# Two expert routers: the inverse root leaves the gathered rows, places come from two matmuls, and the first weight pieces are split before the router

## The reference, cut to what matters

```python
def rms_norm(x, g):                                   # first mixture's norm; the second's is the same
    return x * lax.rsqrt(jnp.mean(x * x, axis=-1, keepdims=True) + 1e-6) * g

# first mixture: 4 groups of 8 experts, width 512; a row picks one group and two experts in it
g_logit = h @ w_rg + b_rg;  g_sel = argmax(g_logit);  g_p = softmax(g_logit)[g_sel]
e_logit = (h @ w_re + b_re) of that group;  top_v, top_i = top_k(e_logit, 2)
gate = softmax(top_v) * g_p
out[row] += gate * ((silu(h @ w_gate[e]) * (h @ w_up[e])) @ w_down[e])

# second mixture: 8 experts, width 2816; two of them per row
logits = h @ router_w + router_b;  top_v, top_i = top_k(logits, 2);  gate = softmax(top_v)
out += gate[e] * ((silu(h @ w1[e]) * (h @ w3[e])) @ w2[e])
```

## Time and profile before

| | |
|---|---|
| median of 3 runs | 2421.14 us (2418.27 to 2421.76) |
| profiled execution, its own time | 2415.43 us |
| its span | 2413.6 us |
| PE busy, share of the span | 95% |
| DVE busy | 76% |
| ACT busy | 61% |
| mean DMA rate | 256 GB/s over the span |

### The profile page before, as it was taken

The page is one execution under the profiler, slowest core; times in us unless marked ns, Lnnn a source line. Parts: engine busy times, 40 slices in busy tenths (PEclk is TensorE's granted clock), DMA queues, the critical chain, the costliest instruction groups (busy, mean ns, idle before and its releaser), DMA issues.

```text
span 2413.6 us, 30101 instructions
## 1 busy us (share of the span) xinstructions
PE 2303.7 (95%) x12162; PEld 1877.1 (78%) x12162; DVE 1828.2 (76%) x1897; ACT 1479.5 (61%) x1469; POOL 28.7 (1%) x33
## 2 busy tenths in 40 slices
PE   7989998999999998988999998899999999999997
PEld 6777877888888887776788776678888888888885
DVE  5875658888888887766454577687988878888885
ACT  5345537777777776545443654477776767777765
POOL 0100000000000000010000001000000000000000
PEclk9989998999999999999999999899999999999999
DMA  9434445999999997606455551279999989999991
GB/s 231 129 108 149 151 158 192 363 366 358 369 355 369 355 370 251 208 4 199 155 194 170 167 164 62 83 256 362 355 358 367 357 298 348 359 365 356 367 342 65
DMA packets 281223, 617.57 MB, mean 256 GB/s; under 512 B 31849, under 2 KB 130409, under 8 KB 243697
## 3 DMA queue, kind: packets, MB, share of 16 engines
q1 hardware_dynamic: 279664, 611.33, 73.5%
q10 hardware_dynamic: 1408, 4.19, 0.4%
HBM read 612.34 MB, written 1.05 MB: 254 GB/s over the span
## 4 chain that ended last, share of the span: by engine, by line
PE 86%; DVE 9%; ACT 4%; issue 2%; DMA 0%; DVEq 0%; ACTq 0%; SPq 0%
PE ps L569 25%; PE ps L570 25%; PE ps L571 24%; DVE ring_parts L593 3%; PE ps L2162 1%; ACT high_parts L589 1%; PE ps L2843 1%; PE ps L2132 1%; PE ps L3132 1%; PE ps L2133 1%; DVE arena L3389 1%; PE ps L2176 0%; PE ps L675 0%; PE ps L2177 0%; PE ps L1082 0%
## 5 line engine op out<-in xcount | busy, mean ns | idle before, releaser
L593 DVE TENSOR_TENSOR ring_parts<-ring,high_parts 128x2048 fp32r<-128x2048 f32 (+1 forms) x574 | 1283.1, 2274 | 172.7 <-ACT high_parts L589 172.2
L589 ACT CAST high_parts<-ring 128x2048 fp32r<-128x2048 f32 (+1 forms) x574 | 1078.6, 1897 | 185.3 <-PE ps L571 181.1
L571 PE MATMUL ps<-high_parts,arena_parts 128*128 128x512 f32 (+2 forms) x1560 | 618.5, 396 | 0.0
L569 PE MATMUL ps<-high_parts,hT_parts 128*128 128x512 f32 (+2 forms) x1120 | 455.7, 407 | 28.2 <-DVE ring_parts L593 9.8
L570 PE MATMUL ps<-ring_parts,hT_parts 128*128 128x512 f32 (+2 forms) x1120 | 444.2, 397 | 0.0
L569 PE MATMUL ps<-high_parts 128*128 128x512 f32 x912 | 365.2, 400 | 0.0
L570 PE MATMUL ps<-ring_parts,high_parts 128*128 128x512 f32 x912 | 359.3, 394 | 0.0
L571 PE MATMUL ps<-high_parts 128*128 128x512 f32 x912 | 356.5, 391 | 0.0
L571 PEld LDWEIGHTS ps<-high_parts,arena_parts 128*128 128x128 f32 x1560 | 298.9, 192 | 68.7
L569 PE MATMUL ps<-high_parts,arena_parts 128*128 128x512 f32 x744 | 294.5, 396 | 7.2 <-DVE arena_parts L1878 2.9
L570 PE MATMUL ps<-ring_parts,arena_parts 128*128 128x512 f32 x744 | 293.8, 395 | 0.0
(11 more groups left out here) (533 smaller groups left out, 1791.3 us busy)
## 6 DMA issues: line engine op xcount, KB each, us to landing
ring<-in_moe_w SPq DMA_DIRECT2D x248, 1024.0 KB, 5.2
ring<-in_w_gate SPq DMA_DIRECT2D x64, 1024.0 KB, 5.5
ring<-in_w_up SPq DMA_DIRECT2D x64, 1024.0 KB, 5.4
ring<-in_w_down SPq DMA_DIRECT2D x64, 1024.0 KB, 5.3
ring<-in_w_in SPq DMA_DIRECT2D x104, 256.0 KB, 4.4
ring<-in_ffn_w SPq DMA_DIRECT2D x44, 512.0 KB, 4.9
ring<-in_w_in SPq DMA_DIRECT2D x20, 1024.0 KB, 5.7
ring<-in_moe_w SPq DMA_DIRECT2D x32, 512.0 KB, 5.0
```

The costliest lines, as they stand in the source:

```text
L569: pe.matmul(dst, a_hi, b_hi, start=first, stop=False, skip_group_check=True)
L571: return pe.matmul(dst, a_lo, b_hi, start=False, stop=last, skip_group_check=True)
L589: act.copy(high_flat(p), raw_flat(p)).then_inc(upper, 1)
L593: dve.tensor_tensor(raw_flat(p, ring_parts_flat), raw_flat(p), f32(high_flat(p)), ALU.subtract).then_inc(split, 1)
```

## The change

In words:

- ACT's copy `m_xh` and DVE's `m_xl` are made from `x*g` without `rstd`, one half of the columns at a time: `upper_rows_act` and `lower_rows_dve`, each two instructions of 128x512 per half. The left half is done before the last add into `x`, the right half after it.
- `rstd` is multiplied into both gates (`two_gates`), and stands as one more column of `gate_w`, so that the small gate matmuls bring it to the gathered rows; Silu takes it as its scale. For the very first step two further small matmuls bring it, ahead of the gates.
- The running counts take two matmuls and four small DVE operations; the count of the fullest bucket is made after the selection (`count_dve`).
- In `gather` the three chunks that open the banks do all their high products first, a row tile at a time, so that they can start before the low rows are there; `up` waits for each chunk of rows as it needs it, not for all eight.
- The first two weight pieces of each expert layer are split before the router: on ACT at the places where the hooks of the output projection stand, on DVE one after q = 1 (second layer: before q = 0) and one between the adds q = 2 and q = 3 (`behind`). The high buffers are dealt out in another order so that these are free in time.
- After the last add DVE multiplies by the gain first and copies the transposes after it; ACT squares first and copies after it. In the second router a quarter of the router's matmuls (row tile 1 of the left half) stands behind the last transposes.

The core of the diff:

```diff
@@ evacuate
                         copy(j, ps[:, j.bank, 0:j.n]).then_inc(evac_act if engine == "act" else evac_dve, 1)
+                        if behind:
+                            behind(eng, j)
@@ first_act: out_hook
                 if i == n_ab + 13 and phase:
                     moe_gain_act(act, moe1)
+                    act.wait_ge(used, pieces_of["out_1"][1].n + 1)
+                    split_high(act, moe1.plan[0].up[0])
                 if i == n_ab + 14 and phase:
                     evac_half(act, "act", "n2", g2T, None, 0, (2, 3))
-                    norm_half_act(act, 0)
+                    act.wait_ge(used, pieces_of["out_1"][2].n + 1)
+                    split_high(act, moe1.plan[0].up[1])
+                    norm_half_act(act, 0, nt_squares)
+                    upper_rows_act(act, moe1, 0)
@@ first_dve
+                if i == n_ab + 13 and phase:
+                    split_low(dve, moe1.plan[0].up[0])
+            def out_behind(dve, j):
+                if j.q == 2:
+                    split_low(dve, moe1.plan[0].up[1])
+                    lower_rows_dve(dve, moe1, 0)
-            evacuate(dve, "out_1", "dve", lambda j, src: out_copy(dve, j, src), hook=out_hook)
+            evacuate(dve, "out_1", "dve", lambda j, src: out_copy(dve, j, src), hook=out_hook, behind=out_behind)
+            dve.wait_ge(evac_dve, jobs_of["out_1"][-1].evac)
+            moe_gained_dve(dve, moe1, 1)
             evac_half(dve, "dve", "n2", g2T, None, 1, (6, 7))
-            moe_gained_dve(dve, moe1, 1)
@@ router_pe
-            for t in range(NT):
-                pe.matmul(ps[:, 6, t * nb:(t + 1) * nb], causal_up[:], r_hit[:, t, 0:nb], start=True, stop=(t == 0))
-                if t:
-                    pe.matmul(ps[:, 6, t * nb:(t + 1) * nb], ones[:], r_hit[:, t - 1, 0:nb], start=False, stop=True)
-            for t in range(NT):
-                mm = pe.matmul(ps[:, 6, NT * nb:(NT + 1) * nb], ones[:], r_hit[:, t, 0:nb], start=(t == 0), stop=(t == NT - 1))
-            mm.then_inc(sig("placed"), 1)
+            pe.matmul(upto, causal_up[:], hit, start=True, stop=True)
+            pe.matmul(total, ones[:], hit, start=True, stop=True).then_inc(sig("placed"), 1)
@@ place_dve
+            dve.tensor_copy(r_place[:, 1, 0:nb], total[:, 0, :])
+            vstep(dve, dve.tensor_tensor(r_place[:, 0, 0:nb], upto[:, 0, :], r_hit[:, 0, 0:nb], ALU.mult))
+            vstep(dve, dve.tensor_tensor(r_place[:, 1, 0:nb], r_place[:, 1, 0:nb], upto[:, 1, :], ALU.add))
+            vstep(dve, dve.tensor_tensor(r_place[:, 1, 0:nb], r_place[:, 1, 0:nb], r_hit[:, 1, 0:nb], ALU.mult))
@@ two_gates
+            vstep(dve, dve.tensor_tensor(r_c[:, 7], r_c[:, 7], rstd[:], ALU.mult))
             vstep(dve, dve.tensor_tensor(r_c[:, 8], r_c[:, 7], r_c[:, 5], ALU.mult))
...
+            for t in range(NT):
+                dve.tensor_copy(gate[:, t, :, f.e], rstd[:, t:t + 1].to_broadcast([P, f.buckets]))
+                first, second = [oh[:, t].rearrange("p (b k) -> p b k", k=f.e) for oh in (oh1, oh2)]
+                ins = dve.tensor_tensor(gate[:, t, :, 0:f.e], first, second, ALU.add)
@@ router_norm_act, and the new functions
-            norm_half_act(act, 1)
+            norm_half_act(act, 1, nt_squares)
+            evac_half(act, "act", PLAIN[f.number - 1], g2T if f is moe1 else gain_of(1, 1), None, 1, (6, 7) if f is moe1 else (2, 3))
             norm_root_act(act, n)
-            act.wait_ge(sig("rstd"), n + 1)
+            upper_rows_act(act, f, 1)
+        def upper_rows_act(act, f, half):
+            cols = slice(512 * half, 512 * half + 512)
+            act.wait_ge(sig("moe_xg"), 4 * (f.number - 1) + 2 * half + 2)
             for t in range(NT):
-                act.wait_ge(sig("moe_xg"), 4 * f.number)
-                ins = act.mul(m_xh[:, t, :], nt_xn[:, t, :], rstd[:, t:t + 1])
-            ins.then_inc(sig("moe_xh"), 1)
+                act.copy(m_xh[:, t, cols], nt_xn[:, t, cols]).then_inc(sig("moe_xh"), 1)
+        def lower_rows_dve(dve, f, half):
+            cols = slice(512 * half, 512 * half + 512)
+            for t in range(NT):
+                dve.wait_ge(sig("moe_xh"), 4 * (f.number - 1) + 2 * half + t + 1)
+                dve.tensor_tensor(m_xl[:, t, cols], nt_xn[:, t, cols], f32(m_xh[:, t, cols]), ALU.subtract).then_inc(sig("moe_xl"), 1)
@@ moe_main_pe: gather
-                pe.wait_ge(sig("moe_sel"), k + 1)
-                pe.wait_ge(sig("moe_xl"), f.number)
...
+                for t in range(NT):
+                    pe.wait_ge(sig("moe_xh"), 4 * (f.number - 1) + 2 + t + 1)
+                    pe.wait_ge(sig("moe_sel"), NT * k + t + 1)
+                    for c in range(3):
+                        upper(c, t)
+                if b == 0:
                     for t in range(NT):
+                        pe.matmul(ps[:, TURN, 0:1], f32(m_sel[:, t, 0:P]), rstd[:, t:t + 1], start=(t == 0), stop=(t == NT - 1))
+                for t in range(NT):
+                    pe.wait_ge(sig("moe_xl"), 4 * (f.number - 1) + 2 + t + 1)
+                    for c in range(3):
+                        lower(c, t)
+                for c in range(3, KC):
+                    pe.wait_ge(sig("moe_rows"), KC * k + c - 2)
+                    for t in range(NT):
+                        upper(c, t)
+                        lower(c, t)
@@ moe_main_pe: up
+                    if gathered is not None:
+                        pe.wait_ge(sig("moe_rows"), KC * gathered + c + 1)
@@ moe_main_act: silu
-                act.activation(m_sg[:, 0:st.n], ps[:, GATE, 0:st.n], ACT.Silu).then_inc(sig("moe_silu"), 1)
...
+                act.activation(m_sg[:, 0:st.n], ps[:, GATE, 0:st.n], ACT.Silu, scale=scale).then_inc(sig("moe_silu"), 1)
@@ moe_main_dve
             select(0)
+            lower_rows_dve(dve, f, 1)
+            count_dve(dve, f)
@@ out_part (second router)
                     if slot == 7 and l:
-                        router_half_pe(pe, moe2, 0)
+                        router_half_pe(pe, moe2, 0, (0,))
...
                     turn_half(pe, x, 1, (2, 3))
+                    router_half_pe(pe, moe2, 0, (1,))
...
+                def behind(dve, j):
+                    if l and j.q == 2:
+                        lower_rows_dve(dve, moe2, 0)
+                        split_low(dve, moe2.plan[0].up[1])
```

More of the change, by code:

```diff
@@ L627, in pe_project, with evacuate @@
                         each(pe, j)
[L629 removed]
+        def evacuate(eng, name, engine, copy=None, norm=None, hook=None, x_done=None, behind=None):
             if norm is not None:
@@ L723, in norm_whole_act, with norm_half_act @@
             ins.then_inc(sig("norm_sq"), 1)
-        def norm_half_act(act, half):
+        def norm_half_act(act, half, squares=None):
             for t in range(NT):
                 cols = slice(half * 512, (half + 1) * 512)
-                ins = act.activation(nt_sq[:, t * 512:(t + 1) * 512], x[:, t, cols], ACT.Square, accum_out=half_sums[half][:, t:t + 1])
+                sq = nt_sq[:, t * 512:(t + 1) * 512] if squares is None else squares[:, t, cols]
+                ins = act.activation(sq, x[:, t, cols], ACT.Square, accum_out=half_sums[half][:, t:t + 1])
             if half:
@@ L974, in emit @@
         group_m.high_at = spare - 2 * PIECE
+        M_HIGH = [0, 0, 0]
+        for k in range(3):
+            M_HIGH[(n_ab + 13 + k) % 3] = spare - k * PIECE
         def highs(*starts):
             return [high_parts[:, a - HI_BASE:a - HI_BASE + PIECE] for a in starts]
-        group_m.high = highs(spare, spare - PIECE, spare - 2 * PIECE)
+        group_m.high = highs(*M_HIGH)
         for l in range(LAYERS):
@@ L1554, in emit, with router_half_pe @@
         assert MR.at <= MR_AT + MR_SIZE
-        def router_half_pe(pe, f, half):
+        def router_half_pe(pe, f, half, tiles=(0, 1)):
             w, n = (r1_w, 36) if f is moe1 else (r2_w, NE2)
             xT_ready(pe, PLAIN[f.number - 1], half)
-            for t in range(NT):
+            for t in tiles:
                 for c in range(4 * half, 4 * half + 4):
@@ L1734, in emit @@
         m_rows = [(e_hT, e_hT_lo)] + [tuple(a[:, :, q, :] for a in m_rows3) for q in range(TOGETHER - 1)]
-        moe1.group.high = moe2.group.high = [MX.take(PIECE) for _ in range(HIGH)]
+        lot = [MX.take(PIECE) for _ in range(HIGH)]
+        moe1.group.high = moe2.group.high = [lot[k] for k in (2, 1, 0, 3, 4)]
         MF = Arena(arena)
@@ L2025, in moe_act_bucket @@
                 act.wait_ge(*m.at("gu", g * f.steps + k + 1))
-                act.activation(e_sg[:, k % 2, :], ps[:, 2 + k % 2, 0:FB], ACT.Silu).then_inc(m("silu"), 1)
+                act.wait_ge(*m.at("places", g + 1))
+                act.activation(e_sg[:, k % 2, :], ps[:, 2 + k % 2, 0:FB], ACT.Silu, scale=e_gate[:, f.e:f.e + 1]).then_inc(m("silu"), 1)
                 act.wait_ge(*m.at(f"down{f.slots[k]}_ready", 16 * (g * f.fills[f.slots[k]] + f.nth[k])))
@@ L2267, in rows @@
```

(4 more changed lines are left out.)

120 lines of the change are left out of this document (69 added, 51 removed).

## The result

The changed kernel took **2427.24 us** (median of 11 runs, 2424.51 to 2430.84), the kernel before beside it 2421.10 (11 runs, 2413.39 to 2422.48): ratio 1.0032 [1.0022, 1.0041], slower by 0.3%. Forecast were 2426.1 and a range of 2420.5 to 2429.5. Its profiled execution took 2425.64 us, span 2423.9.

What follows compares the result with a forecast made beforehand. PE was taken to bound the expert streams, and its waits for small things the routers. Second layer's start +4.95, second gather +0.6, first router -0.5 sum to +5.05 us: 2426.1 us, range 2420.5 to 2429.5.

Steps and rivals of the forecast that it cites:

- The late add, +3.8 and +2.2: Second router: q = 3's add comes late, last transposes start +3.8 us later; lower clock from there to the logits, +2.2.
- Logits to gather, -1.7: Second router: fewer count instructions and an earlier PE start shorten logits to gather from 7.47 to 5.75 us, -1.7.
- Gather to weights, +0.65: Second layer: wait for DVE's last row goes, a bank stall comes; gather to first weight matmul 11.7 us against 11.05.
- Sum at the second layer: +4.95 forecast: Second layer's start: 3.8+2.2-1.7+0.65 = +4.95 us later, bounds +2.4 and +6.
- Second gather, +0.6: Second gather (1963.67): weights start 0.5 us earlier, but the second piece's split comes later; +0.6, bounds -0.5 and +1.2.
- First router, -0.5: First router: gather and weights about 1.6 us earlier, mostly lost to a new 1.2 us gate wait; -0.5, bounds -2.0, +0.5.
- Silu's scale, 0: Silu on ACT: a pointer scale adds 84 ns to each of 80 Silus, hidden in ACT's waits; 0, ceiling 6.7 us.
- Rival D: Silu's pointer scale lies on the path: +5+6.7, 2432.8 us; chance 0.04.
- rival A: Second router: the clock holds at full level until the logits; second start +2.4, sum +2.5, 2423.6 us; chance 0.24.
- rival B: Second router: last add is not late, so +3.8 and +2.2 fall away; sum -2.3, 2418.8 us; chance 0.09.
- rival C: First router lacks 0.3 us of room and gates starve PE, +0.5 each; second layer at upper bound; 2428.6 us; chance 0.08.
- the median is 5.7 above that execution: Whole kernel: the runs' median lies 5.7 us above the profiled execution (2415.43); the same step carried 2420.5 to 2426.1.

Runs made afterwards that it cites:

- e9: Kernel before in the changed kernel's SBUF layout (gate_w of 36 columns, HI_AT 10632), old order of high buffers; 2422.75 us, ratio 1.0031.
- e8: Changed kernel with HI_AT 10640, the second router's last two adds together and the first router's gates up to the Exp early; 2403.63 us, ratio 0.9939.
- e6: Changed kernel with HI_AT 10640 and the second router's last two adds together; 2405.42 us, ratio 0.9943.
- e4: Kernel before with Silu's scale read from a column of ones; 2421.18 us, ratio 1.0002.
- e3: Changed kernel with the second router's last two adds together again; 2421.89 us, ratio 1.0015.
- e10: Kernel before with gate_w of 36 columns and HI_AT 10640, high buffers 96 bytes further in all; 2406.77 us, ratio 0.9957.
- e5: Kernel before with only its high buffers 64 bytes further (HI_AT 10640), gate_w unchanged; 2429.93 us, ratio 1.0048.
- e1: Kernel before with only its high buffers and gathered rows 32 bytes further (HI_AT 10632); 2426.50 us, ratio 1.0035.
- e2: Changed kernel with its high buffers 32 bytes further than in it (HI_AT 10640); 2410.23 us, ratio 0.9969.

## Why the prediction was right, and where not

The number was right, and the steps in the two routers were too; that the total fitted so well was in part luck, as the end of this section shows. Each term is compared first with the profile of before, from which it was worked out, then with e9, which has the layout of after. The left half's last transposes ahead of the second router, from which I count, and e9's rows behind them:

```profile
1551.51 1.04 PE L675 MATMUL ps<-ident,x 128*128 128x128 f32 x8
```

```profile
1553.14 1.04 PE L675 MATMUL ps<-ident,x 128*128 128x128 f32 x8
...
1558.49 1.07 PE L675 MATMUL ps<-ident,x 128*128 128x128 f32 x8
1560.62 3.31 PE L1561 MATMUL ps<-r_w,hT 128*128 128x8 f32 x16 [1.06 <-DVE hT L693]
...
1571.41 0.82 PE L2132 MATMUL ps<-arena_parts 128*128 128x512 f32 x1 [2.02 <-DVE arena_parts L2349]
...
1582.39 0.50 PE L569 MATMUL ps<-high_parts,hT_parts 128*128 128x512 f32 x1 [1.53 <-DVE high_parts L2359]
```

The first is before's, the others are e9's.

**The late add, +3.8 and +2.2.** Right in kind, a little large. Transposes moved from 1556.89 to 1562.39; the profile of after was already 1.98 us late at its left half's transposes (1553.49 against 1551.51), so +3.5, and the same against e9 (1562.39-1558.49-0.35). To the logits (1564.15+5.13) 6.9 us instead of 4.06: +2.8, which I had as the upper bound, since the transposes and all 24 records of the router's matmuls ran at the lower clock. But in e9 too the clock fell behind the transposes, without any late add: its 16 records took 3.31 us against 1.92, and the whole way 5.44. Against e9 it is +1.45. This is the term that was sized too large: part of the slow stretch was charged to the idle time though the old routers have it in other executions.

**Logits to gather, -1.7.** 1569.28 to 1575.01 is 5.73 us (forecast 5.75), against 7.47 before and 7.48 in e9.

**Gather to weights, +0.65.** 1575.01 to the first weight matmul at 1586.2 is 11.2 us, against 11.05: +0.15 (e9 11.0: +0.2). Its parts are as listed, with the stall at 1.11 (forecast 1.1 to 1.3) in place of the wait of 1.53. The clock had risen some 3 us into the gather, the earlier of the two cases that I had worked out and the one that gave 11.2.

**Sum at the second layer: +4.95 forecast.** Against the profile of before it is 1586.2-1579.47-1.98 = +4.75. But in e9, with the old routers, the first weight matmul stands at 1582.4 and its left half's transposes at 1553.14, 0.35 before those of after: only +3.5. The clock of 1550 to 1590 was 0.83 there and 0.87 in the profile of before. So some 1.2 us of the difference to that profile is clock that the old routers lose in other executions as well, the 1.4 us in the router's matmuls above.

**Second gather, +0.6.** +0.8 to +0.9: from the gather's start to the gates it is 16.26 us in after (1971.90 to 1988.16), 15.42 in e9 and 15.36 in before; the wait for the bank is 1.0 and one for the second piece's split 0.9, where I had 1.2 and nearly none.

**First router, -0.5.** Right in mechanism: the transposes stayed where they were in e9 (360.49), the gather came 1.6 us earlier, and the new wait for the gates was 1.33 (forecast 1.2). The gather itself took longer, so the first weight matmul was only 0.9 us earlier (382.69 against 383.61), not 1.6. Net of after against e9, by SyncE's DMA issues near 405 us, about -0.1: the wait took back nearly all. e8 against e6 puts the wait and the slow matmuls behind it together at about 1.8 us (overlapping ranges), which with the -0.1 comes near the bound of -2.0.

**Silu's scale, 0.** Right (e4), with 669-578 = 91 ns each instead of the 84 from a cast and an activation of half the size. The Trainium skill (ScalarE: Activation LUTs, What ACT_TABLE_LOAD costs) gives about 93 ns for a pointer operand; the rows agree with it better than with my pair.

**The rivals.** Rival D is refuted by e4, rival A by PEclk 0.54 in 1560 to 1570, and rival B's mechanism by the wait of 4.31 us. Of rival C neither half came: the first router's transposes weren't late, and its net was -0.1 and not +0.5. e3 and e6 are rival B made true: 2421.89 against 2422.75 in e9, 2405.42 against 2406.77 in e10, that is -0.9 and -1.4, where it was priced at -2.3; the ranges overlap in both pairs.

The routers together are +3.5 to +4.5 by the pairs, and 3.5+0.8-0.1 = +4.2 by the rows of after against e9, the step between their spans too; forecast +5.05. One sum in the forecast was wrong: with all lower bounds together (+2.4, -0.5, -2.0) the terms reach down to 2421.0, not 2423.6; the range of 2420.5 to 2429.5 held that all the same.

**What the prediction lacked** is the layout. It put a wider `gate_w` and a moved `HI_AT` at nothing, without a reason. In the profiled executions the sum is 2425.64-2415.43 = +10.2, twice the forecast; 4.2 of it is the step from e9 to after (spans 2419.7 and 2423.9), the other 6 that from before to e9, all in paces and clock. The median moved by only 6.1, and here my step "the median is 5.7 above that execution" helped without being understood. The executions of before lie in two groups, 2413.0 to 2416.6 and 2418.3 to 2423.9; its profile is of the lower one, the first median of 2421.14 of the upper. In the runs of before beside the experiments the granted clock of the whole execution is 0.978 to 0.983 in the lower group and 0.974 to 0.979 in the upper. There is no profile of before in the upper group; e4, whose edit cost nothing, stands in for it. The two profiles differ in the clock of the mixer and the router ahead of the second layer. Before (us, PE busy, clock, DMA share, GB/s):

```profile
1400.00:1500.00 100.00, 89.60 (x1256) 1.00 0.37 117
1500.00:1550.00 50.00, 43.05 (x252) 0.93 0.18 59
1550.00:1590.00 40.00, 32.24 (x155) 0.87 0.32 107
```

and e4, whose profiled execution took 2422.75 with nothing but the Silu changed:

```profile
1400.00:1500.00 100.00, 91.33 (x1248) 0.97 0.36 118
1500.00:1550.00 50.00, 42.27 (x248) 0.90 0.14 45
1550.00:1590.00 40.00, 32.25 (x144) 0.79 0.22 75
```

The changed kernel has no such lower group: all of its runs but one lie between 2424.51 and 2427.62. So the layout costs 2 to 8 us, by whether the upper or the lower group of before is compared with e9 (2421.40 to 2424.69); the ratio of e9 over a mixture says 0.3%. That is the luck in the number: the total came right because the routers were priced 0.5 to 1.5 too high and the layout's share was left out, while the median compared with was mostly of before's upper group. How the layout acts stays open. The traces speak against the splits of ScalarE and VectorE as the whole cause, for the pace differs in the short pieces in which both engines are idle as well. Two such pieces at the same place of the stream, of e5 and of e10 (busy and count of PE, PEld, DVE, ACT, POOL; clock, DMA share, GB/s):

```profile
549.19:550.08 0.89, 0.89 (x6) 0.70 (x5) 0.00 (x0) 0.00 (x0) 0.00 (x0) 1.00 0.91 350
```

```profile
546.66:547.45 0.79, 0.79 (x6) 0.64 (x5) 0.00 (x0) 0.00 (x0) 0.00 (x0) 1.00 0.92 373
```

The same three intervals from L570 on take 0.72 us in e5 (549.35 to 550.07) and 0.68 in e10 (546.75 to 547.43); over all such pieces of the three expert stretches, some 90 intervals in each trace, the mean is 237 ns in e5, 231 in before and 226 in e10 (it doesn't follow the counts everywhere: 231 in e1 too, whose count is 1983). PE's own reads and the DMA's writes are among what is left, and no run parts them. Nor is it shown what sends an execution of before into one group or the other.

## What to carry to other kernels

- Where two results that share a buffer's release are added one behind the other, put no long work between the adds: 3.6 us of rows and split stood in front of what PE waited for, and the transposes behind the idle time ran at the lower clock (1.97 us against 1.09 in e3). Order within the engine, not the amount of work, made the difference (e3).
- A change that alters the size of an allocation is two changes. Build the old kernel in the new layout (here the width of `gate_w` and `HI_AT`) before judging the work; count matmuls in a stretch where PE never waits, which shows a pace to 0.05% (traces of one layout differed by 1 matmul in 2000).
- A term worked out from one profile holds for that execution's clock. Look for groups among the runs' times before the gap between the profile and the median is carried along.

## What was not expected of the hardware

The pace of back-to-back 128x512 matmuls with split fp32 operands, in stretches at full clock and without any wait, depended on where SBUF buffers lie, in steps of 32 bytes: 450 us held 1982 to 2015 of them (0.2270 to 0.2233 us each, transposes included), a spread of 1.7%. The lowest and the highest count (e5, e10) are 32 bytes apart, by which everything behind `gate_w` moved; against the changed kernel's layout the fast one is worth 16 to 17 us of 2420 (e9 to e10, after to e2). The Trainium skill (SBUF — State Buffer, SBUF: two separate sides) says that TensorE, ScalarE and VectorE's own ports never wait on anyone, with contention between engines only at the ports that VectorE shares with GpSimd. GpSimd does nothing in these stretches (0.00 us), and the rows above fit it as far as they go, since the layouts differ where ScalarE and VectorE are idle too. A dependence of PE's pace on the place of a buffer isn't in that rule; the runs show one, and not whether anything waits at a port.
